# The prompt's peer_v rows: 104 of each token's 128 summed by token in TensorE, the other 24 summed by expert in VectorE, in a transformer step on one core

## The reference

```python
u = jnp.take(expert_u, ib, axis=0)
a = gelu(jnp.einsum('nd,nhkd->nhk', xb, u))
coef = (a * wb)
out = jnp.einsum('nhk,nhkd->nd', coef, jnp.take(expert_v, ib, axis=0))
```

## Time and profile before

| | us |
|---|---|
| median of 3 runs | 4706.99 |
| lowest, highest | 4700.55, 4713.91 |
| profiled execution | 4705.42 |
| its span | 4703.6 |

### The profile page before, as it was taken

One profiled execution on the slowest core, in us unless ns is written; L12 is line 12 of the kernel. 1 busy time (PEld: TensorE's weight loads), 2 busy tenths in 40 slices (PEclk: granted clock), 3 DMA queues, 4 the chain that ended last, 5 costly groups with the idle time before them and its releaser, 6 DMA issues.

```text
span 4703.6 us, 31737 instructions
## 1 busy us (share of the span) xinstructions
PE 3582.2 (76%) x10776; PEld 1650.1 (35%) x10776; DVE 2945.2 (63%) x3905; ACT 646.2 (14%) x1545; POOL 1521.1 (32%) x1102
## 2 busy tenths in 40 slices
PE   4879989999799899999999893000122799999892
PEld 0333434444344444444444341000111444444341
DVE  2322027988333302377768979999999856666568
ACT  0111001100132200111110110000455400000000
POOL 0000003543333100243443466556555222222224
PEclk7989999999899999999999897555555899999996
DMA  9998998999999889899999999999998799999997
GB/s 378 383 350 296 358 348 335 356 355 357 375 410 409 323 284 337 333 366 363 364 371 416 370 409 421 393 366 378 362 383 350 263 394 393 421 421 421 421 421 316
DMA packets 385245, 1736.67 MB, mean 369 GB/s; under 512 B 26432, under 2 KB 30048, under 8 KB 231248
## 3 DMA queue, kind: packets, MB, share of 16 engines
q0 software_dynamic: 150336, 1079.53, 57.1%
q1 hardware_dynamic: 234768, 655.39, 36.6%
HBM read 1703.00 MB, written 33.13 MB: 369 GB/s over the span
## 4 chain that ended last, share of the span: by engine, by line
PE 34%; DMA 29%; DVE 26%; issue 9%; ACT 1%; POOL 1%; SPq 0%; DVEq 0%; POOLq 0%; PEldq 0%; ACTq 0%
PE ps L938 25%; DVE big L2251 9%; DMA big<-in_peer_u,sel 5%; DMA big<-in_peer_v,sel 4%; DMA zone<-in_peer_u,sel 3%; DMA zone<-in_peer_v,sel 3%; DMA big<-in_w_in 3%; DVE activations L2286 2%; DMA big<-in_w_ada 2%; PE ps L1038 2%; DMA big<-in_peer_v,zone 2%; PE ps L1097 2%; DVE big L1907 2%; DVE big L1968 1%; DVE work L1822 1%
## 5 line engine op out<-in xcount | busy, mean ns | idle before, releaser
L938 PE MATMUL ps<-big,activations 128*128 128x512 f32 x4032 | 1768.5, 599 | 51.7 <-DMA big<-in_w_in 14.0
L938 PEld LDWEIGHTS ps<-big,activations 128*128 128x128 f32 x4032 | 766.2, 192 | 1036.5 <-issue 980.4
L910 POOL DMA_INDIRECT big<-in_peer_u,sel x256 | 413.9, 1617 | 312.2 <-DVE qts L2251 126.1
L1331 PE MATMUL ps<-ident,zt 128*128 128x128 f32 x3 | 0.9, 426 | 451.4 <-DVE zt L2225 451.4
L1968 DVE CUSTOM_DVE_ANT_0 big<-big 128x2048 f32<-128x2048 f32 x128 | 289.3, 2290 | 43.5 <-DMA big<-in_peer_u,sel 42.0
L884 POOL DMA_INDIRECT big<-in_peer_u,sel x128 | 217.8, 1701 | 285.4 <-DVE zone L1968 248.5
L1907 DVE SCALAR_TENSOR_TENSOR big<-big,work 128x2048 f32<-128x2048 f32 x115 | 270.5, 2352 | 62.7 <-DMA big<-in_peer_v,sel 59.3
L1897 DVE CUSTOM_DVE_ANT_0 big<-big 128x2048 f32<-128x2048 f32 x114 | 259.6, 2289 | 71.2 <-DMA big<-in_peer_u,sel 70.3
L2251 DVE CUSTOM_DVE_ANT_0 big<-big,zone 128x2048 f32<-128x2048 f32 x128 | 287.0, 2283 | 0.6 <-DVE activations L1929 0.2
L2251 DVE CUSTOM_DVE_ANT_0 big<-big,activations 128x2048 f32<-128x2048 f32 x128 | 287.0, 2283 | 0.4
L2286 DVE SCALAR_TENSOR_TENSOR activations<-big,work,activations 128x2048 f32<-128x2048 f32 x79 | 185.7, 2351 | 114.1 <-DMA big<-in_peer_v,sel 113.7
(11 more groups left out here) (268 smaller groups left out, 4420.3 us busy)
## 6 DMA issues: line engine op xcount, KB each, us to landing
big<-in_w_in SPq DMA_DIRECT2D x84, 2048.0 KB, 11.6
big<-in_w_ada SPq DMA_DIRECT2D x48, 2048.0 KB, 12.1
big<-in_w_out SPq DMA_DIRECT2D x24, 2048.0 KB, 12.0
big<-in_peer_w_query SPq DMA_DIRECT2D x24, 2048.0 KB, 10.1
misc<-in_peer_v SPq DMA_DIRECT2D x43, 1024.0 KB, 9.1
zt<-in_peer_v SPq DMA_DIRECT2D x43, 1024.0 KB, 9.2
zone<-in_peer_v SPq DMA_DIRECT2D x42, 1024.0 KB, 9.1
big<-in_w_branch_a SPq DMA_DIRECT2D x12, 2048.0 KB, 9.6
```

Of the source, the lines that this page charges most:

```text
L910: pool.indirect_dma_start(u_slot(m), None, eu, bass.IndirectOffsetOnAxis(ap=sel[:, t % 2, k:k + 1], axis=0)).then_inc(u_in[m % UR], 16)
L938: ins = nc.tensor.matmul(bank(bk), acts[:, k, b * P:(b + 1) * P], w[:, n % WS, k], start=(start and k == 0), stop=(stop and k == KT // 2 - 1))
```

## The change

POOL's gather of token n brings the first 104 rows only (`BY_TOKEN = P - ROWS_0`), and PE's `token(n)` contracts over 104 partitions. The last 24 experts of all tokens (`ROWS_0 = 24`) are gathered by expert, 128 rows of 8 KB each, into the four ring slots. POOL issues these 24 gathers behind the 128 gathers by token; ahead of the first stand waits for both early gate products (`mm_done`, `U_BR[1] + 2`) and for ScalarE's third evacuation of the branch part (`bank_free`, `U_BR[1] + 3 + NB`). VectorE adds them to `acc` with the coefficient column of `coef_0`, eight ahead of each of the merges 1, 2 and 3. Their indices are copied out of `idx_0` once, into `row_ids`. The constants on `ring_free` and `ring_in` move by 24. The diff, without the six places where only such a constant changes (LATE_AT, SP's last wait, the loop of gathers, `gelus`, the two in `peer_step`):

```diff
@@ -102,6 +102,8 @@
 VR_0 = 6
+ROWS_0 = 24
+BY_TOKEN = P - ROWS_0
@@ -189,6 +191,7 @@
+        ids_0 = sb("row_ids", [P, ROWS_0], u32)
@@ -887,13 +890,18 @@
-                        pool.indirect_dma_start(v_slot_0(n), None, ev, bass.IndirectOffsetOnAxis(ap=idx_t0[:, n:n + 1], axis=0)).then_inc(v_in[n % VR_0], 16)
+                        pool.indirect_dma_start(v_slot_0(n)[0:BY_TOKEN], None, ev, bass.IndirectOffsetOnAxis(ap=idx_t0[0:BY_TOKEN, n:n + 1], axis=0)).then_inc(v_in[n % VR_0], 16)
+                    pool.wait_ge(mm_done, U_BR[1] + 2)
+                    pool.wait_ge(bank_free, U_BR[1] + 3 + NB)
+                    for i in range(ROWS_0):
+                        pool.wait_ge(ring_free, 2 * P + i + 1)
+                        pool.indirect_dma_start(slot(i), None, ev, bass.IndirectOffsetOnAxis(ap=ids_0[:, i:i + 1], axis=0)).then_inc(ring_in[i % RING], 16)
@@ -1035,8 +1043,8 @@
-                        ins = nc.tensor.matmul(ps[32 * j:32 * j + 32, 7 * 512:8 * 512], spread_0[q % 2][:, i * 32:(i + 1) * 32],
-                                               v_slot_0(n)[:, j * CH:(j + 1) * CH], start=(i == 0), stop=(i == 31))
+                        ins = nc.tensor.matmul(ps[32 * j:32 * j + 32, 7 * 512:8 * 512], spread_0[q % 2][0:BY_TOKEN, i * 32:(i + 1) * 32],
+                                               v_slot_0(n)[0:BY_TOKEN, j * CH:(j + 1) * CH], start=(i == 0), stop=(i == 31))
@@ -1975,6 +1983,7 @@
+                            link(V.tensor_copy(ids_0[:, :], idx_0[:, BY_TOKEN:P]))
@@ -2169,10 +2178,23 @@
+                ROWS_BEHIND = [range(n * ROWS_0 // (DCH - 1), (n + 1) * ROWS_0 // (DCH - 1)) for n in range(-1, DCH - 1)]
+                ROWS_BEHIND[0] = ()
+
+                def row_0(i):
+
+                    if i == 0:
+                        dve.wait_ge(fa_in, 32)
+                    dve.wait_ge(ring_in[i % RING], 16 * (P // RING + i // RING + 1))
+                    signal(V.scalar_tensor_tensor(acc, slot(i), coef_0[:, BY_TOKEN + i:BY_TOKEN + i + 1], acc, ALU.mult, ALU.add),
+                           ring_free, RING + 2 * P + i + 1)
+
                 if g < 2:
                     for c in range(DCH):
                         if g == 0 and c % 2:
                             ada((A_BR + 2 * c) // 4)
+                        for i in ROWS_BEHIND[c] if g else ():
+                            row_0(i)
                         merge(c)
```

More of the change, by code:

```diff
@@ L264, in slot @@
             return bg(G0 + (j % RING) * D, D)
-        LATE_AT = (2 * PH - 2) * 2 * TOPK
+        LATE_AT = (2 * PH - 2) * 2 * TOPK + ROWS_0
         def late_slot(i):
@@ L773, in _ @@
                         sp.dma_start(scd[:, at:at + CH], zn((v % 4) * CH, CH)).then_inc(G["sc_st"][v % 4], 16)
-            sp.wait_ge(ring_free, RING + 2 * PH * 2 * TOPK)
+            sp.wait_ge(ring_free, RING + 2 * PH * 2 * TOPK + ROWS_0)
             sp.dma_start(fin_x, x1d[0]).then_inc(fa_in, 16)
@@ L895, in _ @@
                         for q in range(2):
-                            gathers(g, i * 2 + STEP0[g] + q, q, i * (4 * TOPK) + (PH + q) * 2 * TOPK)
+                            gathers(g, i * 2 + STEP0[g] + q, q, i * (4 * TOPK) + (PH + q) * 2 * TOPK + ROWS_0)
                     for q in range(2):
@@ L1389, in gelus @@
             def gelus(g, at):
-                sa.wait_ge(ring_free, at + RING + TOPK)
+                sa.wait_ge(ring_free, at + ROWS_0 + RING + TOPK)
                 nc.scalar.activation(gel, dots, ACT.Gelu).then_inc(ge_done, 1)
@@ L1887, in arrived @@
                     if late is None:
-                        dve.wait_ge(ring_in[k % RING], (m * (32 // RING) + (k // RING + 1 - P // RING)) * 16)
+                        dve.wait_ge(ring_in[k % RING], (m * (32 // RING) + (k // RING + 1 - (P - ROWS_0) // RING)) * 16)
                     else:
@@ L1907, in peer_step @@
                     signal(V.scalar_tensor_tensor(acc, tile(TOPK + k), coef[:, k:k + 1], acc, ALU.mult, ALU.add),
-                           ring_free, m * 32 + RING + TOPK + k + 1)
+                           ring_free, m * 32 + ROWS_0 + RING + TOPK + k + 1)
                     if during:
```

## The result

| | us |
|---|---|
| before, median of 4 | 4706.49 |
| after, median of 4 | 4970.48 (4962.87 to 4987.61) |
| after / before | 1.0565, 95% interval 1.053 to 1.06 |
| span of the profiled execution, before and after | 4703.6, 4961.2 |

The change costs 264 us where I forecast 22, and the time lies 224 us above my range.

The account below looks back on a forecast made before the run. No engine bounds throughout: the DMA decides from 1250 to 1290 us, PE in the later attention and branch part. 36 us lost minus 14 gained is 22 more than 4705.4, 4727, as median 4729 us; range 4702 to 4746.

Parts of the forecast that it names:

- The attention's gain: Attention: shorter gathers cut PE's waits by 5.6 us, 7.0 us and 1 us of key waits; 14 us gained, bounds 0 and 31.
- The first rival: Attention: the shorter gathers are no faster, the waits stay and only the branch part's 36 us loss is left; 4743 us, 13%.
- turning the 13 engines: Attention gathers: 104 rows split over 13 engines, eight rows each, changing from gather to gather; if so, the 14 us stand.
- PE's products over 104 partitions: Attention: PE's token matmuls lose 24 of 128 rows; 19 us if time followed rows, but nothing taken.
- The most that could go: Attention: upper bound of the gain if all PE's waits go, 14.9 + 7.0 + 9.6 = 31 us.
- The branch part: Branch part: new gathers delay PE's weights; 23 + 12 + 1 = 36 us lost, bounds 6 and 61.
- the first burst's landings: Branch part, ahead of chunk 1: 12 gathers take 39 us; weight halves land at 1692 and 1709.4 us; 23 us lost.
- the low clock: Branch part: PE starts at a low clock after a wait for weights, 1.6 us more each time.
- the third burst: Branch part: the last 4 gathers delay a half, there at 22.5 us and wanted at 21.6; 1 us lost.
- The rival by which the weights keep their rate: Branch part: halves land in time beside gathers, 6 to 15 us lost, attention gains 14; 4699 to 4708 us, 20%.
- VectorE and POOL at nothing: Branch part: VectorE's 24 additions, 19 us ahead of each of three merges, are hidden; POOL's work also costs nothing.
- that sign: Branch part: the prediction is wrong if weight halves land in under 15 us beside the gathers.

## Why the prediction was wrong, step by step

**The attention's gain: the step that failed.** I took 0.6 us off each token by dividing bytes by the stage's rate, 416 GB/s, and set the worst case at "nothing, if shorter gathers take as long as the full ones". The gather's rate belongs to its shape: 104 rows come at half of it. The term was +14 us with bounds of 0 and 31; it measured -217.6 us by itself. I had written that no row shows a gather of this shape, and still bounded it on one side as if fewer bytes could not be dearer. The nearest row gave a price for 128 rows alone, and nothing in the trace bounded the other side. A rule of the Trainium skill against this change I had not weighed: by its port map ("SBUF — State Buffer", section "Door 1: The DMA port swizzle") 104 rows put as many rows on the fullest port as 128 do. By that nothing is gained, and in the runs no gather of 52 to 120 rows from partition 0 on gained anything; the loss of 218 us is more than the map says. Why 104 rows cost 0.62 us and not the floor's 0.39 stays open.

**The first rival** ("the shorter gathers are no faster") stood next to the truth and stopped at zero gain. The Trainium skill's rule that I cited beside it ("DMA: Bandwidth & Descriptors", section "Why a DMA increments its semaphore by 16 and not by 1") is borne out in its count: gathers of 104 rows leave 13 four-byte packets at their end (and 27 ahead of their rows), those of 128 rows 16, in the records of the kernels with one in flight. My reading of it, that turning the 13 engines would keep the rate, is not: 104 rows ran at 0.62 us a row, and 112 and 96, which divide into 16 engines, at 0.53.

**PE's products over 104 partitions**: nothing taken, and rightly. Their shortest is 589 ns with 104 rows and 590 with 128.

**The most that could go**, 31 us of waits, was not exceeded by gathers that are not slow: 64 rows brought 31 us of the whole time spread and 25 us on partitions 32 to 95.

**The branch part**: 36 us forecast, 45.4 in the changed kernel, 44.3 with full gathers by token. By chunk, from PE's starts: 93.25 - 64.72 = 28.5 us up to chunk 2 (forecast 23), 55.56 - 44.04 = 11.5 (forecast 12), 48.91 - 43.53 = 5.4 (forecast 1). The mechanism is as drawn: two waits ahead of chunk 1, one for the fourth half of chunk 2. The mis-sized terms are the first burst's landings (PE starts on the first half 37.8 us behind the part's start, forecast 33, and on the second 54.1 us behind it, forecast 50.3), the low clock, which I took twice and which came after each of four waits, and the third burst, where PE waited 3.25 us and I had 1 us. My sum for that one was wrong besides: 18 us behind the same 3.5 us is 21.5, not 22.5, which is no loss at all by my own terms. The rival by which the weights keep their rate falls: PE waits four times for `in_w_in`, 43 us in all, and once more 1.46 us for `in_w_branch_a`. I had called the prediction wrong if halves landed in under 15 us, and their median is 14.6; that sign was badly chosen, since the median takes in the halves that load between the bursts, and the first one in a burst took 38.5.

**VectorE and POOL at nothing**: right, by the idle time ahead of the merges.

**The total**: -14 + 36 was written, +223 + 45 came.

## What to carry to other kernels

Don't shorten a gather's partitions to save bytes: on partitions from 0 on, 120, 112, 104 or 96 rows took 0.53 to 0.66 us of engine time each where 128 rows took 0.31, so the full gather is over before the shorter one; if fewer rows are wanted, 64 on partitions 32 to 95 or on every second one did save here (25 and 31 us). Where an edit gives a transfer a shape that the trace doesn't hold, leave its price open upward and time that shape alone first; one run of it settles a change like this. And bytes moved into a stage that lives on one load ahead of the matmul cost there what the burst delays, here 1.7 to 2.0 us for each 1 MB gather, even where average bandwidth is free: even with gathers of ideal rate, 31 us at the very most stood against 45.

## What the runs showed of the hardware

- Gathers of 8 KB rows into SBUF: engine time of a row 0.31 us with 128 rows on 128 partitions, 0.53 with 96 or 112 rows, 0.57 with 120, 0.62 to 0.66 with 104, 0.63 with 64, 0.86 with 52, each on neighbouring partitions from 0.
- The same 64 rows on every second partition 0.39 us, on partitions 32 to 95 0.40 us, in a queue that is not full; a full gather alone in flight shows 0.39 too. 128 rows as two gathers on every second partition: 0.31 us; as two halves: 0.55 us.
- With a full queue the DMA share stays at 0.9 to 1.0, fast or slow. Only the rate beside it shows the loss, from 1300 to 1550 us 410 GB/s in the mean with 128 rows and 205 to 254 with 96 to 120.
- The other queue's loads slow down with it: 512 KB of `z_blocks` landed after 10.3 us beside gathers of 128 rows and after 18.8 beside those of 104 (1300 to 1550 us of both kernels).
- A gather of 104 rows leaves 40 packets of four bytes (8315 packets less 49.15 MB / 8192, over 57.7 gathers), one of 128, 112 or 96 rows 16, one of 120 rows 24, one of 52 rows 28.
- The first 16 rows of a gather of 128 that is alone in flight took 0.78 us each in the mean, the other 112 took 0.33. A gather of 16 rows to partitions 0 to 15 was through in 0.76 us in the median, though by the full queue's 0.314 us a row four ways would need 1.26.
